# VectorE's order inside the expert loop: the low half of the gated units ahead of its part of a weight tile's low half

## The reference, cut to what matters

```python
def expert(acc, ew):
    wg, wu, wd, cw = ew
    hid = jax.nn.silu(t @ wg) * (t @ wu)
    return acc + (cw[:, None] * (hid @ wd)).astype(acc.dtype), None
```

## Time and profile before

| | |
|---|---|
| median of 3 timed runs | 2509.26 us (2508.42 to 2522.15) |
| the profiled execution | 2514.59 us, its span 2512.9 us |
| mean granted TensorE clock in the span | 0.94 of full speed |
| TensorE matmul busy | 2159.1 us (86%) |
| VectorE busy | 1591.7 us (63%) |
| ScalarE busy | 1115.9 us (44%) |
| GpSimd busy | 475.6 us (19%) |
| expert loop of the first layer | about 458 to 650 us of the span |
| expert loop of the second layer | about 968 to 1168 us of the span |

### The profile page before, as it was taken

The page is one execution under the profiler, slowest core; times in us unless marked ns, Lnnn a source line. Parts: engine busy times, 40 slices in busy tenths (PEclk is TensorE's granted clock), DMA queues, the critical chain, the costliest instruction groups (busy, mean ns, idle before and its releaser), DMA issues.

```text
span 2512.9 us, 40162 instructions
## 1 busy us (share of the span) xinstructions
PE 2159.1 (86%) x15258; PEld 1899.4 (76%) x15268; DVE 1591.7 (63%) x2540; ACT 1115.9 (44%) x1628; POOL 475.6 (19%) x328
## 2 busy tenths in 40 slices
PE   5999886788489776876899999889997999899997
PEld 2776465677377475765878999779996899888997
DVE  2878655577468555764566776666667666556665
ACT  3224533566333634674444455224332433455332
POOL 1000002688300016884042021100000000000000
PEclk7999898899789888998899999999998999999999
DMA  6457812799445136995325467455543445333452
GB/s 253 168 202 270 283 67 92 275 344 342 169 150 197 39 118 238 329 324 212 134 101 210 169 211 240 163 187 186 191 175 134 143 175 209 123 113 118 177 192 82
DMA packets 103173, 471.48 MB, mean 188 GB/s; under 512 B 11520, under 2 KB 30208, under 8 KB 66048
## 3 DMA queue, kind: packets, MB, share of 16 engines
q1 hardware_dynamic: 84480, 404.79, 45.4%
q0 software_dynamic: 13232, 44.84, 4.7%
q10 hardware_dynamic: 5328, 20.07, 2.0%
HBM read 412.76 MB, written 54.79 MB: 186 GB/s over the span
## 4 chain that ended last, share of the span: by engine, by line
PE 42%; DVE 6%; ACT 2%; issue 1%; DVEq 1%; SPq 1%; DMA 0%; POOL 0%; ACTq 0%; POOLq 0%
PE bank L754 12%; PE bank L756 12%; PE bank L755 12%; DVE ring_halves L424 2%; ACT high L1428 1%; PE bank L1149 1%; PE bank L1283 1%; PE bank L1335 1%; PE bank L805 1%; PE bank L1316 1%; PE bank L1273 1%; PE bank L1260 1%; DVE dring_halves L433 0%; PE bank L1265 0%; PE bank L1264 0%
## 5 line engine op out<-in xcount | busy, mean ns | idle before, releaser
L754 PE MATMUL bank<-ssdb_halves,high 128*128 128x256 f32 (+1 forms) x2080 | 619.5, 298 | 51.1 <-DVE HT_halves L1967 18.6
L755 PE MATMUL bank<-HT_halves,high 128*128 128x256 f32 (+1 forms) x2096 | 619.6, 296 | 0.0
L756 PE MATMUL bank<-ssdb_halves,ring_halves 128*128 128x256 f32 (+1 forms) x2080 | 616.6, 296 | 0.0
L424 DVE TENSOR_TENSOR ring_halves<-ring,high 128x2048 fp32r<-128x2048 f32 (+1 forms) x230 | 482.3, 2098 | 195.6 <-ACT high L1428 194.4
L1428 ACT CAST high<-ring 128x2048 fp32r<-128x2048 f32 x230 | 437.5, 1903 | 217.6 <-PE bank L756 121.2
L754 PEld LDWEIGHTS bank<-ssdb_halves,high 128*128 128x128 f32 x2080 | 396.2, 190 | 70.7 <-issue 37.1
L755 PEld LDWEIGHTS bank<-HT_halves,high 128*128 128x128 f32 x2096 | 402.1, 192 | 8.9
L756 PEld LDWEIGHTS bank<-ssdb_halves,ring_halves 128*128 128x128 f32 x2080 | 396.5, 191 | 10.3
L424 POOL TENSOR_TENSOR ring_halves<-ring,high 128x1024 fp32r<-128x1024 f32 x66 | 224.7, 3404 | 651.7 <-ACT high L1428 651.7
L433 DVE TENSOR_TENSOR dring_halves<-dring,dhigh 128x1024 fp32r<-128x1024 f32 (+1 forms) x152 | 226.3, 1489 | 159.6 <-ACT dhigh L1434 159.1
L1434 ACT CAST dhigh<-dring 128x1024 fp32r<-128x1024 f32 x152 | 160.6, 1057 | 243.9 <-PE bank L756 243.9
(11 more groups left out here) (453 smaller groups left out, 3888.1 us busy)
## 6 DMA issues: line engine op xcount, KB each, us to landing
ring<-in_ffn SPq DMA_DIRECT2D x88, 1024.0 KB, 5.6
ring<-in_moe SPq DMA_DIRECT2D x64, 1024.0 KB, 7.4
ring<-in_ada SPq DMA_DIRECT2D x48, 1024.0 KB, 6.1
dring<-in_ffn_down SPq DMA_DIRECT2D x88, 512.0 KB, 3.7
dring<-in_moe_down SPq DMA_DIRECT2D x64, 512.0 KB, 4.7
ring<-in_foxin SPq DMA_DIRECT2D x24, 1024.0 KB, 4.9
ring<-in_win SPq DMA_DIRECT2D x22, 1024.0 KB, 7.7
zs_b<-x_slots POOLq DMA_DIRECT2D x32, 512.0 KB, 8.9
```

What stands on the lines that cost most here:

```text
L424: eng.tensor_tensor(low, w, h, ALU.subtract).then_inc(sem(f"low_{engine}"), 1)
L754: mm(o, a[0], b[0], start=first, stop=last and bool(kw), **kw)
L755: mm(o, a[0], b[1], start=False, stop=last and bool(kw), **kw)
L756: return mm(o, a[1], b[0], start=False, stop=last, **kw)
```

## The change

In VectorE's slice code the call that makes its part of tile j+2's low half moves from ahead of the low half of the gated units to behind it. Nothing else differs; the other engines' lists are the same.

```diff
                     dve.wait_ge(sem("gate_act"), act0 + j + 1 + RING * g)
                     tt(hrows[:, j % 2, :], gact[:, j % 2, 0:P], ps[4 + j % 2][:, P:TCOLS], ALU.mult).then_inc(sem("hid_raw"), 1)
-                    if j + 2 < slices:
-                        make_low(dve, "dve", c0 + j + 2, g)
                     dve.wait_ge(sem("hid_high"), hid_high0 + j + 1 + RING * g)
                     tt(r(hid[:, j % 2, 1, 0:P]), ps[4 + j % 2][:, TCOLS:TCOLS + P], hid[:, j % 2, 0, 0:P], ALU.subtract)\
                         .then_inc(sem("hidden"), 1)
+                    if j + 2 < slices:
+                        make_low(dve, "dve", c0 + j + 2, g)
                     if j % 2 == 0 and j // 2 + 1 < blocks:
                         split_rows(j // 2 + 1, g)
```

## The result

The changed kernel takes 2636.74 us (median of 4 runs, 2634.15 to 2644.55) against 2509.43 us before it (median of 4 as well): 127 us more, a ratio of 1.050 with a 95% interval of 1.046 to 1.054. The profiled execution took 2637.57 us, its span is 2635.9 us, 123 us more than the 2512.9 us before. The prediction was 2546 us in a range of 2537 to 2598: the sign was right, the size was not, and the time lies outside the range.

What follows compares the result with a forecast made beforehand. Expert blocks were taken as bound by a 12.34 us cycle through ScalarE's copy-out and GpSimd's subtraction; 15 blocks x 2 layers x 1.23 us = 37 us on 2509.26 gave 2546 us, range 2537 to 2598.

Steps and rivals of the forecast that it cites:

- Steps 1 to 5: Even slice: line 2399 early, GpSimd takes the shared port pair first, VectorE's 424 and line 2390 late; 1.23 us per block.
- Step 6: Odd slice: line 424's later wait is covered; VectorE's down-tile part and GpSimd's next subtraction tie at 513.09, winner left open.
- The likeliest case: Expert loops: GpSimd gets the first turn, VectorE wins the tie; 37 us added, 2546 us, chance 0.38.
- the bound above: Expert loops: GpSimd also wins the tie, another 1.5 us per block; 2.73 x 30 = 82 us, 2591 us.
- The case with both turns lost: VectorE loses its weight subtraction's and down-tile part's turns to GpSimd in all blocks; 82 us, 2591 us, chance 0.22.
- A: Even slice's turn flips to GpSimd, VectorE wins the tie; 2546 us, chance 0.38.
- B: Turn flips and GpSimd wins the tie: all blocks 2591 us, chance 0.22; about half of them 2569 us, chance 0.18.
- the cycle: Expert block: copy-out, silu, high half, GpSimd's subtraction, TensorE, next copy-out; 12.34 us a block, delays count one for one.
- The table-load block of those rows: Second layer: a 1.28 us table load between copy-out and silu; block 13.8 us against about 12.1 to 12.3 without.
- C: Even slice: the turn does not flip, VectorE's 424 still goes first, 0.38 us longer per block; 2521 us, chance 0.12.
- D: Even slice: GpSimd starting on an idle pair does not block VectorE; 0.68 us faster per block, 2489 us, chance 0.05.
- E: Nothing measurable: the edit frees a wait that another covers, line 2390 on time; 2509 us, chance 0.05.

Runs made afterwards that it cites:

- filled run: Changed kernel plus 18 and 8 useless identity transposes around the first half of `gate_up` in odd-numbered slices, filling TensorE's two waits; 2599.83 us, ratio 1.0318.
- rows first: Changed kernel with `split_rows` (line 2390) placed ahead of VectorE's part of the weight tile in even slices; 2531.43 us, ratio 1.0062.
- who goes first: Changed kernel with GpSimd waiting in even slices for VectorE's part of the same tile's low half; 2552.18 us, ratio 1.0143.
- second turn: Changed kernel with GpSimd's weight-tile part waiting in odd slices for VectorE's down-tile part from the even slice before; 2573.3 us, ratio 1.0204.

## Why the prediction was wrong in size

**Steps 1 to 5, the first turn: right.** Line 2399 came early, the down products' wait fell from 1.26 to 0.29 us and nothing came of it. GpSimd took the pair first: alone it needs 2.38 us (2.39 worked out), VectorE's 424 took 3.15, `gate_up(j+2)` waited 2.53 for line 2390. At full clock this is 1.15 us a block, worked out as 1.23. The Trainium skill, page "SBUF — State Buffer", section "Who interferes with whom", says that the order of issue, not the form of the instruction, decides who is blocked; the trace agrees: VectorE's 424 waited when GpSimd's was ahead (549.83 against 550.14), and GpSimd's waited when VectorE's was (508.46 against 508.51 before the change).

**Step 6, the tie: left open, and the less likely side came.** The likeliest case, 2546 us, had VectorE win it; the chance of GpSimd winning in all blocks was put at 0.22. It won in 29 of 30 blocks, by 0.02 to 0.04 us of start, and in the one left there was no race. The odd slice's own wait was harmless, as said.

**The step that failed is the clock, a term that step 6 and the bound above put at nothing, without a reason.** The case with both turns lost was priced at 2591 us, 2.73 us in each of 30 blocks. At full clock that price is right: 2.71 us a block in the filled run. But it took the clock of the earlier trace rows for granted, while both cases A and B make TensorE wait longer than it did. In the changed kernel the clock falls about 1 us behind the wait of 2.5 us, ahead of the one of 1.0, and stays at the lower level for most of the rest of the block, where the products of `gate_up` follow each other every 0.21 us and not every 0.12. That is 2.2 us in each of the 14 distances between copy-outs of the first layer and in 5 of the second.

The traces add up as follows. The 28 distances are 117 us longer than before the change: 76 us of waits, as in the filled run at full clock, and 41 us of clock. The two first blocks add 2.7 and 1.1 us (in the second nobody raced), which makes 121 of the 123 us by which the spans differ. Between the forecast case with both turns lost (82 us) and the measured 127 us lie 45, and the clock is 41 of them; the other 4 are no more than the runs of one kernel differ by.

The prediction used for one thing, that a delay on the cycle counts in full, and that holds at an unchanged clock. The table-load block of those rows holds TensorE up for 1.74 us at an unchanged clock of 1.00:

```profile
1018.63 0.33 PE L1079 MATMUL bank<-con,border 128*128 128x128 f32 x1 [1.74 <-DVE border L2395]
```

The wait that the prediction itself forecast was longer, 2.6 us. The trace of the kernel before has one as long outside the expert loops, behind 7.9 us in which TensorE was busy almost throughout: TensorE's instruction behind it, and the stretches ahead of it, in it and after it (columns as in the earlier trace rows).

```profile
910.46 1.76 PE L805 MATMUL bank<-wide,con 128*128 128x256 f32 x4 [2.57 <-ACT wide L1456]
```

```profile
900.00:906.00 6.00, 6.00 (x52) 6.00 (x51) 3.20 (x5) 1.91 (x1) 1.79 (x1) 1.00 0.78 281
906.00:908.00 2.00, 1.88 (x16) 1.68 (x14) 0.08 (x1) 0.03 (x1) 1.65 (x1) 1.00 0.89 361
908.00:910.46 2.46, 0.00 (x1) 0.00 (x1) 0.96 (x2) 2.46 (x3) 0.51 (x1) 1.00 0.53 140
911.00:914.50 3.50, 3.50 (x10) 2.76 (x10) 0.13 (x1) 0.97 (x2) 2.34 (x1) 0.54 0.70 288
```

The clock is 0.54 in the 3.5 us after it. So the sign that a wait of the forecast length can cost the clock was there to be read. That the waits bring the clock down is shown by filling them: between the copy-outs it then is 1.00 in both layers. Which pattern of waits is still safe the runs do not settle. With one wait of 1.54 us the clock held (rows first), with one of about 1.9 us it fell in many blocks (who goes first), with one of 2.53 in many too (second turn), and in the second layer of the changed kernel three blocks with both waits kept full clock. Nor does a fall always cost its 2.2 us: of two table-load blocks of 16.5 us in that layer one has a clock of 0.90 (1068.3 to 1084.8) and one of 1.00 (1099.6 to 1116.1).

**The rivals.** C and D are excluded: GpSimd's even 424 takes 2.38 us, and VectorE's waits for it to end. E is excluded by the time, and B is the case that came, with the clock on top.

## What to carry to other kernels

When two engines take turns on one resource, moving an instruction of one by some 0.4 us, as here, can hand the turn to the other; look at what is queued behind the loser, since that is what becomes late, and at the next turn as well. Before shortening a wait, look whether a second one follows it at once: here the second set the time, and moving a copy-out off that chain gained what the edit couldn't. And price a forecast wait on TensorE twice, once as time and once as the clock that may be lost behind it.

## What had not been expected of the hardware

A race decided by 0.02 to 0.04 us fell the same way in all 29 blocks that had it, so a tie in a trace is not to be treated as a coin thrown anew in each block. And TensorE gets through a block in 14.8 us with 26 useless transposes in it, and in 17.0 us without them: two waits of 2.5 and 1.0 us in a block cost 2.2 us more through the clock than their own length.
